# Unread transposes in the opening, the forget gate behind slot 2, ten staging buffers from slot 22, and the last tile's products in two halves

## What is computed

```python
for l in range(DEPTH):          # 2 layers
    h = rmsnorm(x, norm_w[l]);  z = h @ w_in[l]
    gq, gk, gv, gg, glr, rq, rk, rv, rg = split(z)
    la = log_sigmoid(glr @ gla_w2 + gla_b) / 16
    o_a = gated linear attention(gq, gk, gv, la)      # S = exp(la) S + k v
    o_b = retention(rope(rq), rope(rk), rv)           # S = gamma S + k v
    x = x + concat(norm(o_a) * silu(gg), norm(o_b) * silu(rg)) @ w_out[l]
y = rmsnorm(x, final_norm_w)
```

## Times and profile before

| | us |
|---|---|
| median of 3 runs | 1668.95 |
| lowest and highest | 1668.67, 1671.54 |
| the profiled execution | 1668.71 |
| its span, first to last instruction | 1666.9 |
| TensorE busy | 1641.7 |
| VectorE busy | 1064.9 |
| POOL busy | 840.0 |
| ScalarE busy | 618.6 |

### The profile page before, as it was taken

The page is one execution under the profiler, slowest core; times in us unless marked ns, Lnnn a source line. Parts: engine busy times, 40 slices in busy tenths (PEclk is TensorE's granted clock), DMA queues, the critical chain, the costliest instruction groups (busy, mean ns, idle before and its releaser), DMA issues.

```text
span 1666.9 us, 26235 instructions
## 1 busy us (share of the span) xinstructions
PE 1641.7 (98%) x9742; PEld 1346.4 (81%) x9742; DVE 1064.9 (64%) x2388; ACT 618.6 (37%) x1166; POOL 840.0 (50%) x645
## 2 busy tenths in 40 slices
PE   6999999999999999999999999999999999999998
PEld 4788878887788887888878888788887888878886
DVE  7743666867765575547855467767787557784474
ACT  4423444243342343423443234342333424442342
POOL 4443645645455464444544445556554555554455
PEclk9999999999999999999999999999999999999999
DMA  7634657656564474467643566567864466553554
GB/s 266 154 109 110 183 203 221 192 155 169 194 177 128 114 208 133 120 151 160 202 134 97 151 143 196 163 172 188 193 193 132 122 163 158 171 173 103 142 155 142
DMA packets 389136, 268.19 MB, mean 161 GB/s; under 512 B 290704, under 2 KB 293136, under 8 KB 389008
## 3 DMA queue, kind: packets, MB, share of 16 engines
q1 hardware_dynamic: 315136, 131.99, 31.6%
q10 hardware_dynamic: 73872, 134.51, 25.6%
HBM read 219.34 MB, written 47.07 MB: 160 GB/s over the span
## 4 chain that ended last, share of the span: by engine, by line
PE 90%; DVE 4%; DMA 2%; issue 1%; SPq 1%; POOL 0%; ACT 0%; ACTq 0%; POOLq 0%; DVEq 0%
PE bank L733 78%; PE bank L994 2%; PE bank L1000 1%; PE bank L978 1%; PE bank L956 1%; PE bank L798 1%; PE bank L935 1%; SPq L442 1%; DMA region<-in_x_prompt 1%; PE bank L700 1%; DMA out_k_rows<-region 1%; DMA w_stage<-in_w_slots 1%; PE bank L939 1%; PE bank L1011 0%; PE bank L808 0%
## 5 line engine op out<-in xcount | busy, mean ns | idle before, releaser
L274 POOL TENSOR_TENSOR w_lo<-w_stage,w_hi 128x512 fp32r<-128x512 f32 x264 | 371.7, 1428 | 331.3 <-ACT w_hi L267 331.2
L733 PE MATMUL bank<-h_hi,w_hi 128*128 128x512 f32 x1024 | 408.3, 399 | 4.1 <-DVE h_lo L357 4.1
L733 PE MATMUL bank<-h_lo,w_hi 128*128 128x512 f32 x1024 | 399.8, 390 | 0.0
L733 PE MATMUL bank<-h_hi,w_lo 128*128 128x512 f32 x1024 | 399.4, 390 | 0.0
L274 POOL TENSOR_TENSOR w_lo<-ss,w_hi 128x512 fp32r<-128x512 f32 x164 | 224.3, 1387 | 211.2 <-ACT w_hi L267 211.1
L267 ACT ACTIVATE w_hi<-w_stage 128x512 fp32r<-128x512 f32 x264 | 153.8, 624 | 369.1 <-PE bank L733 286.8
L733 PEld LDWEIGHTS bank<-h_hi,w_hi 128*128 128x128 f32 x1024 | 192.4, 188 | 55.4 <-issue 8.1
L733 PEld LDWEIGHTS bank<-h_hi,w_lo 128*128 128x128 f32 x1024 | 192.5, 188 | 41.1
L733 PEld LDWEIGHTS bank<-h_lo,w_hi 128*128 128x128 f32 x1024 | 192.7, 188 | 37.2
L733 PE MATMUL bank<-w_hi,m_hi 128*128 128x512 f32 x512 | 200.6, 392 | 2.0 <-DVE region L1592 2.0
L733 PE MATMUL bank<-w_hi,h_hi 128*128 128x512 f32 x512 | 201.1, 393 | 0.0
(11 more groups left out here) (218 smaller groups left out, 2209.9 us busy)
## 6 DMA issues: line engine op xcount, KB each, us to landing
w_stage<-in_w_slots ACTq DMA_DIRECT2D x264, 256.0 KB, 3.7
ss<-in_w_slots ACTq DMA_DIRECT2D x164, 256.0 KB, 3.6
v_b<-in_w_slots ACTq DMA_DIRECT2D x84, 256.0 KB, 3.7
region<-in_x_prompt SPq DMA_DIRECT2D x32, 512.0 KB, 5.2
out_o_rows<-region SPq DMA_DIRECT2D x64, 256.0 KB, 3.1
region<-out_o_rows SPq DMA_DIRECT2D x192, 64.0 KB, 3.4
xn<-in_x_t SPq DMA_DIRECT2D x16, 512.0 KB, 5.0
out_k_rows<-region SPq DMA_DIRECT2D x32, 256.0 KB, 3.9
```

The source lines that it names most:

```text
L274: pool.tensor_tensor(w_lo[:, r, c], stage(h), w_hi[:, r, c].bitcast(f32), ALU.subtract).then_inc(lo_done, 1)
L733: i = pe.matmul(P[q][:, :], x, y, start=(s == 0 and kk == 0 and c == 0), stop=(s == 3 and kk == 1 and c == 2), skip_group_check=True)
```

## The change

It has five parts.

1. **Unread transposes.** `idle_turns` issues transposes of the identity into PSUM bank X, which nobody reads: 10 ahead of the second pair of `scale_rows`, 18 behind it, and 8 between k = 0 and k = 1 of the first slot.
2. **The opening's order.** ScalarE makes `h_hi` 0 between the splits of halves 0 and 1, and issues the loads of halves 4 and 5 behind `h_hi` 1. In the first block `hT_slot0` goes from behind slot 1 to behind slot 2, so the gate's readers on ScalarE and VectorE come one slot later (`late`). The decode's statistics product goes behind bank 2, POOL splits halves 2 and 3 ahead of the decode's root, VectorE normalises the decode rows at k = 5 instead of k = 7, and the decode's transposes and the gate's expansion move to banks of slots 2 and 3.
3. **VectorE's slots 4 and 5.** The q copy (`queries`) is taken out of `rotate` and put ahead of the second half of the gate's sums.
4. **Ten buffers from half 42** (slot 22) instead of half 48 in a layer's second block.
5. **The tail.** The last tile's products of unit 7 are done in two halves of 256 columns, the second in bank X; each half is added and has its own statistics (`last_quarter`).

```diff
         def buffer(h):
-            return h % HALVES % STAGED if h // HALVES % NBLK == 1 and h % HALVES < 48 else h % STAGES
+            return h % HALVES % STAGED if h // HALVES % NBLK == 1 and h % HALVES < 42 else h % STAGES
...
+        def last_quarter(vec, c):
+            if c == 0:
+                vec.wait_ge(proj.sem, proj.at(LAST, 25))
+            else:
+                vec.wait_ge(slot_used, LAST * SLOTS + SLOTS + RING)
+            y = y_t[:, 3, 512 + 256 * c:768 + 256 * c]
+            vec.tensor_tensor(y, (P[3], X)[c][:, 0:256], y, ALU.add).then_inc(last_half if c == 0 else y_add.sem, 1)
+            vec.wait_ge(last_half, 1) if c == 0 else vec.wait_ge(y_add.sem, y_add.at(LAST, 8))
+            return vec.bn_stats(last_bn[:, 6 + 6 * c:12 + 6 * c], y)
...
+        def idle_turns(pe, count):
+            for _ in range(count):
+                pe.transpose(X[:, 0:128], ident[:, :], ident[:, :])
+
         def scale_rows(pe):
             for t in range(TPB):
                 if t % 2 == 0:
+                    if t > 0:
+                        idle_turns(pe, 10)
                     pe.wait_ge(first_rs, t // 2 + 1)
                 i = pe.transpose(ATT[:, TOK * t:TOK * t + TOK], xrs[:, t:t + 1].to_broadcast([128, 128]), ident[:, :])
             i.then_inc(ht_ps.sem, KT)
+            idle_turns(pe, 18)
...
             for h in range(2):
                 split_lo(pool, h)
+            for h in range(2, 2 * AHEAD):
+                split_lo(pool, h)
             pool.wait_ge(s_v.sem, s_v.at(0, V_NV - V_LAST))
             rsqrt(srs[:, :], svar[:, :], s_p.sem)
-            for h in range(2, 2 * AHEAD):
-                split_lo(pool, h)
...
                     def last_slots():
                         pe.wait_ge(lo_done, DEPTH * NBLK * HALVES)
-                        for q in range(4):
-                            i = products(7, 2, q)
-                            if q == 3:
-                                i.then_inc(slot_used, 1)
-                            products(7, 3, q).then_inc(slot_used if q == 3 else proj.sem, 1)
+                        for q in range(3):
+                            products(7, 2, q)
+                            products(7, 3, q).then_inc(proj.sem, 1)
+                        for c in range(2):
+                            cut = slice(256 * c, 256 * c + 256)
+                            products(7, 2, 3, cut=cut)
+                            i = products(7, 3, 3, cut=cut)
+                            if c == 0:
+                                i.then_inc(proj.sem, 1)
+                        i.then_inc(slot_used, 2)
...
                             products(0, 0, 0, (k,))
+                            if k == 0:
+                                idle_turns(pe, 8)
                         for q in range(4):
                             if q > 0:
                                 i = products(0, 0, q)
-                            if q == 0:
+                            if q == 2:
                                 sample_sum(0)
...
-                            i = products(u, s, q)
-                            if n == 0 and u == 0 and s == 1:
-                                if q == 0:
-                                    sample_transposed(0)
-                                if q == 1:
-                                    gate_expand()
-                                if q == 2:
-                                    sample_gate()
+                            for cut in (slice(0, 256), slice(256, 512)) if n == LAST and u == 7 and q == 3 else (slice(0, 512),):
+                                i = products(u, s, q, cut=cut)
+                            if n == 0 and w == 2 and q == 2:
+                                sample_transposed(0)
+                            if n == 0 and w == 3 and q == 0:
+                                gate_expand()
...
                         if n == 0 and w == 1:
                             first_slot()
-                            hT_slot0()
                             continue
...
+                        if n == 0 and w == 2:
+                            hT_slot0()
...
             split_hi(act, 0)
+            next_hi(act, 0, 0)
             split_hi(act, 1)
-            load_half(act, 4)
-            load_half(act, 5)
-            for k in range(KT):
+            for k in range(1, KT):
                 next_hi(act, 0, k)
-                if k in (3, 5):
-                    split_hi(act, (k + 1) // 2)
+                if k == 1:
+                    load_half(act, 4)
+                    load_half(act, 5)
+                if k in (2, 3):
+                    split_hi(act, k)
...
-                if k == 7:
+                if k == 5:
                     sample_norm(0)
```

75 lines of the change are left out of this document (47 added, 28 removed).

## The result

| | before | after |
|---|---|---|
| median, us | 1668.9 | 1675.16 |
| lowest and highest | 1668.67, 1671.54 | 1674.3, 1676.39 |
| ratio to before, 95% interval | | 1.0035 [1.0022, 1.0048] |
| the profiled execution, its span | 1668.71, 1666.9 | 1674.3, 1672.5 |

Each column has six executions. The changed kernel is 6.3 us slower in the median and 5.6 us in the profiled executions, which the rest of this text compares. The forecast was 1675.7, in a range of 1672.0 to 1681.0. In the changed kernel the lines of the code have moved: L755 is a product (L733 before), L1025 the outputs of slot 20 (L994), L1224 their copies (L1189), L1623 the silu (L1592), L487 the store of the state (L466), L375 the unread transposes.

The account below looks back on a forecast made before the run. TensorE, busy 98% of the span, was taken as the bound. From 1668.7 us, opening -2.7, block 1 -2.0, block 5 +11.6 and tail +0.1 gave 1675.7 us, range 1672.0 to 1681.0.

Parts of the forecast that it names:

- opening, to slot 5: Opening: first slot ends 1.7 us sooner and the wait for x before L700 vanishes, 1.0; -2.7 us, other bound 0.
- block 1, slot 25: Layer 1's second block: ten buffers end ScalarE's load wait, so TensorE's idling for the silu goes; -2.0 us, other bound 0.
- block 5, hold: Layer 2's second block, slot 20: ScalarE's load waits for the state store, so TensorE's outputs start 8.2 us later.
- block 5, clock: Block 5 behind the hold: TensorE's clock falls to half after 8 us idle; costs 2.2 us, bounds 1.5 to 3.0.
- block 5, VectorE's lag at slots 21 to 25: Block 5, slot 25: VectorE's silu stays 2.0 us later than TensorE, against a margin of 0.8; costs 1.2 us.
- tail: Last tile's halved products: gain 0.1 us, cost 0.2; +0.1 us, bounds -0.5 and +0.3.
- VectorE's 12.4 less a margin of 0.8: Block 5: VectorE's statistics and silu end at 1203.4, 12.4 us later; slot 25 has 0.8 us to spare.
- rival (a): Opening: transposes bring no clock, so it is +0.9 us in place of -2.7; whole 1679.3 us; chance 27%.
- the step on the gate: Opening: gate's products moved behind slot 2, so the wait for x from 23.6 to 24.67 goes; -1.0 us.
- (b): Block 5: the store lands late, near 1198.3; +2.8 us, 1678.5 us; chance 12%.
- (c): Block 5: the wait costs nothing, the store having landed by 1187.3; 1664.1 us; chance 4%.
- (d): Block 5: TensorE is held for a part only, some 4 to 5 us; about 1669 us; chance 6%.

Follow-up runs that it names:

- e10_b5_turns: The changed kernel plus 62 unread transposes ahead of slot 20's outputs in block 5; 1675.67 us, 1.0035 of the kernel before.
- e1_th48: The changed kernel with ten buffers from half 48 in both layers, as in the kernel before; 1667.58 us, 0.9984 of the kernel before.
- e7_b_turns: The kernel before plus 10 and 18 unread transposes around the second pair of scale_rows, order unchanged; 1669.14 us, 0.9997 of the kernel before.
- e9_gate1: The changed kernel with block 5's state store ahead of slot 17's x loads, and the gate's low-rank products back behind slot 1; 1667.91 us, 0.9989 of before.
- e4_store19: The changed kernel with block 5's state store ahead of slot 19's eight x loads, behind 24 of 32; 1671.36 us, 1.0009 of the kernel before.
- e3_store17: The changed kernel with block 5's state store moved ahead of slot 17's x loads; 1663.78 us, 0.9965 of the kernel before.

## Why the prediction was right

The sum was 1675.7 and the median 1675.16. The profiled executions, in whose time the sum was worked out, differ by 5.6 us where it has 7.0, so the median flatters it. Term by term, from the profiles:

| term | forecast | measured |
|---|---|---|
| opening, to slot 5 | -2.7 | -2.7 |
| L935's wait in block 0 (not in the sum) | 0 | -0.7 |
| block 1, slot 25 | -2.0 | -2.2 |
| a late transfer at the end of layer 1 (not in the sum) | 0 | +0.4 |
| block 5, hold | +8.2 | +7.3 |
| block 5, clock | +2.2 | +2.7 |
| block 5, VectorE's lag at slots 21 to 25 | +1.2 | +0.9 |
| tail | +0.1 | -0.1 |
| sum | +7.0 | +5.6 |

**Block 5** was the term that decided, and it was read off one row: the store stood at 1189.80 on a queue that the change didn't touch. The forecast put the load 5.7 us behind the store's issue; it passed 4.6 behind, and the issue came 0.2 us later against TensorE's slot 20 than before, which makes the 0.9 of the hold. The gap on TensorE, announced as 8 to 11 us, was 7.13. The three terms add up to 11.6, measured 10.9. But two of them are not what their names say. VectorE's lateness was worked out from ScalarE's copies, whatever TensorE did, and in the four kernels with a hold this chain alone sets slot 25; e10_b5_turns, without the half clock, ends no sooner. The working should have said that hold, clock and lag are one number, VectorE's 12.4 less a margin of 0.8, and that the clock only decides which engine waits. Measured, VectorE's statistics came 11.3 later and the margin was 0.6. The moment at which the clock falls was guessed from the end of the kernel, 4 to 5 us behind the last product. It came 3.0 us into the idle time here, and in other runs it followed idle times of 1.89 to 3.06 us. That guess happened not to matter.

**Block 1** went as written: VectorE's silu comes at 389.07, 6.5 us sooner than in the earlier trace rows, of which 3.4 are the opening's, and slot 25 has no wait. That the term measured 2.2 is the luck of one execution, since in e1_th48 and e7_b_turns the same stall took 3.8 us.

**The opening** gave 2.7 us, and the rise of the clock under transposes, on which rival (a) hung, came. The page that the prediction named, the Trainium skill's "TensorE: Matmul & The Clock Gate", section "Part 4: PE-mode transpose", says that the full clock doesn't engage for transposes. This case's traces disagree twice, at 13.3 in the opening (spacing 0.21, then 0.11) and in the 6.93 us of e10_b5_turns. The first product came at 14.94 (forecast 15.3), and the wait before L700 vanished. The total of 2.7 is not firm: the traces with the old opening start slot 5 at 48.2 to 48.5 us, those with the new one at 45.5 to 46.6. In the step on the gate, a cost of 1.0 for its old place was right for the kernel before and too small for the new opening, where it is 4.1 us (e9_gate1). And the split into -1.7 for the first slot and -1.0 for the gate gave the first slot a worth of its own: the transposes alone brought the old opening nothing at slot 5 (e7_b_turns), and nothing that these runs can tell in the new one. The 0.34 us for `w_lo` at slot 2, which I had covered by a margin of 1 us, did come.

**The tail** was nothing to speak of, as said, though both its parts were larger than forecast: the halves cost TensorE 0.4 us (forecast 0.2) and gave 0.5 behind it (forecast 0.1). **Rivals** (b), (c) and (d) fall with the row at 1189.44: the store was not late, the wait was not free, and it was not partial. The 0.7 us in block 0 and the 0.4 at the end of layer 1 stood in no term; the second is a transfer that comes differently late from trace to trace.

## What to carry to other kernels

When a buffer gets a new owner, look for the slowest thing that must leave it first, and for what stands ahead of that on its queue: a store behind 32 unrelated loads cost 10.9 us here, and moving it made the rest of the change a gain of 0.35% over the kernel before. Cost a hold by the engine that is full behind it, not by the one that idles: TensorE's 3.0 us in e4_store19 were 7.1 on VectorE and 6.7 at slot 25, where the two meet. Making TensorE faster in a stretch that VectorE bounds gave nothing (e10_b5_turns), and a faster first slot gave nothing until what stood behind it had moved (e7_b_turns, e9_gate1). Don't price a stall of two or three microseconds at its own length alone.

## What the runs showed of the hardware

- Transposes that nobody reads raise TensorE's clock (in all ten traces that have them) and held it through 6.93 us (e10_b5_turns): they stood 0.21 us apart at 1.2 GHz and 0.11 at 2.4 GHz. The moment of the rise differs between executions of the same opening. It was 13.3 us in the changed kernel, while the run with the tail undone had 18 transposes in 3.44 us and a first product at 15.36, and the run with the gate behind slot 1 had them in 2.13 us (the two rows, in this order):

```profile
12.10 3.44 PE L375 MATMUL bank<-ident 128*128 128x128 f32 x18
```

```profile
11.97 2.13 PE L375 MATMUL bank<-ident 128*128 128x128 f32 x18
```

- The clock fell behind idle times of 1.89 us (e1_th48), 1.93 (e7_b_turns), 2.89 (e4_store19) and 3.06 (e9_gate1), each time 0.3 to 1.1 us after TensorE had resumed, and did not behind 1.96 us in the kernel before nor behind 2.27 in e10_b5_turns. What decides between these is open. It wasn't tried apart.
- A store of two times 512 KB was passed 4.4 to 6.5 us behind its issue: 6.5 with 24 x loads behind it on the queue (e3_store17), 4.4 with eight (e4_store19), 4.6 with none (the changed kernel). That the loads make the difference is likely and not shown.
